# Non-final matmul chunks visit the PSUM banks in rotation instead of one bank after the other

## The chip, the cores and the metric

The kernel runs on one core of one Trainium2 chip, as one launch. The metric is the device time of that core in microseconds (us); lower is better. "TensorE" or PE is the matrix engine, VectorE is DVE, ScalarE is ACT, GpSimd is POOL and SyncE is SP. PSUM is the accumulator memory that TensorE writes; it has eight banks, and one bank takes an output of 128 x 512 f32.

## What is computed

One layer of a hybrid diffusion backbone: 256 latent tokens and 256 context tokens, model width 2048, everything in f32. Cut to what matters:

```
mod   = silu(c) @ w_mod + b_mod                          # shifts, scales, gates; w_mod 2048 x 12288
proj  = modulate(rms(x) * norm1, shift, scale) @ w_in    # w_in 2048 x 13376, latent and context rows
ssm   = rms(bidirectional_ssd(...) * silu(z)) @ w_ssm_br # 2048 x 2048
attn  = grouped_query_attention(q, k, v) @ w_attn_br     # 2048 x 2048
x_mid = x + gate1 * ((sigmoid(g1)*ssm + sigmoid(g2)*attn) @ w_o)
out   = x_mid + gate2 * (silu(h @ w_gate) * (h @ w_up)) @ w_ffn_out   # hidden width 5632
```

The large products dominate. Each is done with operands split in two, high and low part, and three products are summed: high*high + high*low + low*high. The change touches only the order in which these products are issued.

## The kernel before, in words

**Tiles and chunks.** A weight matrix is read in chunks of 1 MB: 512 columns by 512 rows, the rows lying as 4 tiles of 128 on the partitions (`CK_T` = 4). SP issues one DMA per chunk into one of 4 `raw` slots (L423). ACT makes the high part with one copy (L889, `w_hi`), DVE the low part with one subtraction (L1188, `w_lo`); both have two slots (`SPL` = 2), so chunk p+2 is split when chunk p is through on TensorE, which the semaphore `pe_used` tells. TensorE takes the activations (`act_hi`, `act_lo`, 128 tokens x 128 rows) as the stationary operand and the 512 weight columns as the moving one. Each matmul has its own weight load (LDWEIGHTS, shown as PEld).

**Blocks and banks.** A block is 512 output columns; it takes several chunks, and its sums stay in PSUM over all of them. Phases with latent tokens only have two 128-token tiles and so two banks per block (0 and 1); `kv`, `xb` and `dt` have latent and context tokens and so four banks. `br` and `f1` have two products per block, the first in banks 0 and 1 (chunks 0 to 3), the second in banks 2 and 3 (chunks 4 to 7). The phases in order, as blocks x chunks: kv 2x4, xb 6x4, dt 1x1, q 4x4, c 2x4, z 4x4 and g 8x4 (these two with modulation chunks and attention or SSD steps between), br 4x8, o 4x4, f1 11x8, f2 4x11. Before them stands the modulation phase with a function of its own (`mod_chunk`), which the change leaves alone.

**One chunk on TensorE** is the function `chunk` (L517 to L544): it waits for `hi_ready` and `lo_ready`, then loops over the banks, and for each bank over the 4 row tiles with 3 matmuls each: 12 matmuls per bank in a row (L539, L540, L541). So a chunk is 24 matmuls with two banks and 48 with four. In the first chunk of a block (`first`) the matmuls of each bank are preceded by a wait on `bank_free` (L532, or L530 in block 0, where only the first bank waits, for all earlier ones). In the last chunk (`final`) each bank but the last signals `bank_done` when its twelve are through; the last is told by `pe_used`.

**Evacuation.** After the first chunk of the next block has been split on that engine, the block's banks are copied out in order: by ACT in kv, xb, q, c, z, g (L897, `stage_out`), by DVE in br (L1519, `merge`), o (L1561, `residual`) and f2 (L1613, `finish`), and in f1 by ACT for banks 0 and 1 (L1138) and by DVE for banks 2 and 3 (L1589). Each copy raises `bank_free` by one.

**What sets the order.** Every engine's program is written out by hand in program order; nothing is scheduled by a planner. Waits hold an engine's whole queue.

Of the kernel before, what the change touches and what calls it, by code (L numbers as in the profile page):

```python
# [24 lines left out]
P = 128  # L25
# [70 lines left out]
def lin(values, i):  # L96

    if isinstance(i, int):
        return values[i]
    step = values[2] - values[1]  # L100
    assert all(b - a == step for a, b in zip(values[1:], values[2:]))
    return i * step + (values[1] - step)
# [12 lines left out]
def hybrid_block(nc, a, out):  # L115
    with ExitStack() as outer:
        def sem(name):
            return outer.enter_context(nc.semaphore(name))
# [62 lines left out]
        PS = outer.enter_context(nc.psum_tensor("PS", [P, 8, NB], F32))  # L181
# [96 lines left out]
        bank_done, bank_free = sem("bank_done"), sem("bank_free")  # L278
# [30 lines left out]
        def col(table, p):  # L309
            return [row[p] for row in table]  # L310
# [205 lines left out]
        def _(pe):  # L516
            def chunk(ph, i, p, acts, banks, kt0, first, final):  # L517

                pe.wait_ge(hi_ready, lin(col(ph.index, p), i) + 1)
                pe.wait_ge(lo_ready, lin(col(ph.index, p), i) + 1)  # L520
                s = p % SPL
                n, ks = (64, KT) if ph is p_dt else (NB, CK_T)
                hi_w = w_hi[:, s, :, :].rearrange("p k n -> p (k n)")[:, 0:ks * n].rearrange("p (k n) -> p k n", n=n)
                lo_w = w_lo[:, s, :, :].rearrange("p k n -> p (k n)")[:, 0:ks * n].rearrange("p (k n) -> p k n", n=n)
                for t, b in enumerate(banks):
                    if first:
                        prior = ph.banks.index(b) + 1
                        if isinstance(i, int) and i == 0:
                            if t == 0:
                                pe.wait_ge(bank_free, ph.bank0[0])  # L530
                        else:
                            pe.wait_ge(bank_free, lin(ph.bank0, i) - len(ph.banks) + prior)  # L532
                    dst = PS[:, b, 0:n]
                    toks = slice((t % 2) * P, (t % 2 + 1) * P)
                    for k in range(ks):
                        kt = kt0 + (16 if t >= 2 else 0) + k
                        x_hi, x_lo = acts[0][:, kt, toks], acts[1][:, kt, toks]
                        begin, end = first and k == 0, final and k == ks - 1
                        nc.tensor.matmul(dst, x_hi, hi_w[:, k, :], start=begin, stop=False)  # L539
                        nc.tensor.matmul(dst, x_hi, lo_w[:, k, :], start=False, stop=False)  # L540
                        last = nc.tensor.matmul(dst, x_lo, hi_w[:, k, :], start=False, stop=end)  # L541
                    if final and t < len(banks) - 1:
                        last.then_inc(bank_done, 1)
                last.then_inc(pe_used, 1)  # L544

            act1, act2 = (act1_hi, act1_lo), (act2_hi, act2_lo)
# [1 line left out]
            def plain(ph, i, p):  # L548
                chunk(ph, i, p, act1, ph.banks, p * CK_T, p == 0, p == ph.chunks - 1)
# [64 lines left out]
            for ch in range(4):  # L614
                for d in range(2):
# [3 lines left out]
                             start=True, stop=True).then_inc(d_pe, 1)  # L619
# [57 lines left out]
            def z_step(i):  # L677
                for p, what in enumerate(ORDER["z"]):
                    q = int(what[1])

                    if p == 2:
                        pe.wait_ge(a_qkS, i + 1)
                    if p >= 2:
                        attention_steps(i, p - 2, p - 1 if p < 11 else 11)
                    if what[0] == "m":
                        mod_chunk(p_z, i, p, i * 2 + (8 + q // 4), q % 4)
                    else:
                        chunk(p_z, i, p, act1, LAT, q * CK_T, q == 0, q == 3)
                    if p == 0 and not (isinstance(i, int) and i == 0):
                        mod_turn(i * 2 + 7)  # L690
                    if p == 6:
                        mod_turn(i * 2 + 8)
                    if p == 0:
                        attention_start(i)
# [76 lines left out]
            def g_step(i):  # L771
                conv_in(i)
                for p, what in enumerate(ORDER["g"]):
                    q = int(what[1])

                    if p in (1, 4, 6, 7):
                        {1: decays, 4: back_to_rows, 6: states, 7: outputs}[p](i)
                    if what[0] == "m":
                        mod_chunk(p_g, i, p, i + 16, q)
                    else:  # L780
                        chunk(p_g, i, p, act1, LAT, q * CK_T, q == 0, q == 3)
                    if p == 0:
                        mod_turn(i + 15)
# [876 lines left out]
```

## Time and profile before

| | |
|---|---|
| device time, median of 3 runs | 2692.27 us (2691.65 to 2692.89) |
| span of the profiled execution | 2691.1 us |
| TensorE busy (matmuls) | 2370.1 us, 88% of the span, 10239 matmuls |
| DVE / ACT / POOL busy | 1339.0 / 1057.4 / 71.5 us |
| the three matmul lines of `chunk` | 2592 matmuls each, 400 to 406 ns each |
| mean granted TensorE clock | 0.949 of full speed |
| HBM | 169 GB/s over the span |

How to read it: matmuls are pipelined, so a record of 0.40 us overlaps the next one. What counts is the distance from one start to the next, here called the pitch. A timeline row gives start, duration, engine, line, operation and operands; in brackets stands idle time before it and what ended it. A clock of 1.0 stands for 2.4 GHz and 0.5 for 1.2 GHz.

### The profile page before, as it was taken

Reading aid. Unit: us, or ns where it says so; the run is one execution under the profiler, and the core shown is the slowest. Engines: PE = TensorE matmul, PEld = TensorE weight load, DVE = VectorE, ACT = ScalarE, POOL = GpSimd, SP = SyncE. Lnnn points to the kernel's source line nnn. Section 1 sums busy time; section 2 is a strip of 40 time slices with the busy share of each in tenths; the row PEclk is TensorE's granted clock in tenths of the full one; section 3 lists DMA queues with packets and bytes.
Section 4 is the critical chain, followed back from the end, with each engine's and each line's share of the span. In section 5 each row is a group of like instructions: output and inputs, shape, how many; then the busy total and the mean of one; then the engine's idle time right before and its main releaser. Section 6 shows DMA issues by size and latency. Waiting matters only on the chain. (4 is left out here: it accounts for less than half of the span.)

```text
span 2691.1 us, 27845 instructions
## 1 busy us (share of the span) xinstructions
PE 2370.1 (88%) x10239; PEld 1865.6 (69%) x10239; DVE 1339.0 (50%) x1346; ACT 1057.4 (39%) x956; POOL 71.5 (3%) x111
## 2 busy tenths in 40 slices
PE   3689999979887877888778889999799999999999
PEld 2467888877655655666666667778688888877777
DVE  4752222123565555777676755554544444444333
ACT  4532222123355444444444434333444444443332
POOL 0000000000100001000000000000000000000000
PEclk9999999969989898999999989999899999999999
DMA  7933333216745555454444455645455555554553
GB/s 266 311 117 125 110 125 109 102 63 208 212 150 193 168 179 165 156 169 154 154 154 159 151 215 188 206 144 196 148 181 187 187 179 182 184 182 174 183 185 135
DMA packets 225435, 454.32 MB, mean 169 GB/s; under 512 B 11732, under 2 KB 14532, under 8 KB 224104
## 3 DMA queue, kind: packets, MB, share of 16 engines
q1 hardware_dynamic: 202704, 399.01, 43.2%
q0 software_dynamic: 8240, 32.12, 3.8%
q10 hardware_dynamic: 14440, 22.50, 2.3%
q8 instruction: 33, 0.54, 0.1%
q14 instruction: 18, 0.15, 0.0%
HBM read 429.47 MB, written 24.13 MB: 169 GB/s over the span
## 5 line engine op out<-in xcount | busy, mean ns | idle before, releaser
L1188 DVE TENSOR_TENSOR w_lo<-raw,w_hi 128x2048 fp32r<-128x2048 f32 x381 | 871.8, 2289 | 1008.6 <-ACT w_hi L889 1008.3
L539 PE MATMUL PS<-w_hi,act_hi 128*128 128x512 f32 (+1 forms) x2592 | 1051.7, 406 | 93.4 <-DVE w_lo L1188 60.6
L889 ACT ACTIVATE w_hi<-raw 128x2048 fp32r<-128x2048 f32 x381 | 726.9, 1910 | 902.0 <-PE PS L541 855.3
L540 PE MATMUL PS<-w_lo,act_hi 128*128 128x512 f32 (+1 forms) x2592 | 1037.5, 400 | 0.0
L541 PE MATMUL PS<-w_hi,act_lo 128*128 128x512 f32 (+1 forms) x2592 | 1035.8, 400 | 0.0
L539 PEld LDWEIGHTS PS<-w_hi,act_hi 128*128 128x128 f32 x2592 | 503.6, 194 | 239.8 <-issue 89.6
L541 PEld LDWEIGHTS PS<-w_hi,act_lo 128*128 128x128 f32 x2592 | 503.0, 194 | 119.1
L540 PEld LDWEIGHTS PS<-w_lo,act_hi 128*128 128x128 f32 x2592 | 503.7, 194 | 115.5 <-issue 1.7
L569 PE MATMUL PS<-w_hi,c 128*128 128x512 f32 x384 | 175.6, 457 | 117.3 <-DVE w_lo L1188 112.6
L569 PEld LDWEIGHTS PS<-w_hi,c 128*128 128x128 f32 x384 | 79.8, 208 | 163.5 <-issue 142.1
L570 PE MATMUL PS<-w_lo,c 128*128 128x512 f32 x384 | 165.2, 430 | 0.0
L570 PEld LDWEIGHTS PS<-w_lo,c 128*128 128x128 f32 x384 | 81.2, 211 | 16.6 <-issue 1.2
L1435 DVE SCALAR_TENSOR_TENSOR cv<-cin,conv_w,cv 128x256 f32<-128x256 f32 x224 | 91.5, 480 | 2.1 <-DVE cv L1433 0.2
L897 ACT ACTIVATE stage<-PS 128x512 f32<-128x512 f32 x68 | 39.2, 595 | 82.1 <-PE PS L541 80.7
L354 ACT ACTIVATE act_hi<-tmp 128x512 fp32r<-128x512 f32 x40 | 25.3, 632 | 84.5 <-DVE tmp L368 49.7
L1000 ACT ACTIVATE probs<-PS,ast 128x512 f32<-128x512 f32 x32 | 22.0, 689 | 74.0 <-DVE ast L1362 74.0
L738 PEld LDWEIGHTS PS<-tri,a_loc 128*128 128x128 f32 x256 | 33.6, 190 | 15.3 <-issue 15.3
L1065 ACT ACT_TABLE_LOAD x8 | 10.3, 1283 | 77.8 <-DVE cv L1435 77.7
L993 ACT ACTIVATE pT<-PS 128x512 f32<-128x512 f32 x32 | 19.1, 596 | 50.2 <-PE PS L637 50.2
L1484 DVE TENSOR_TENSOR dec<-PS,eacum 128x512 f32<-128x512 f32 x16 | 10.3, 687 | 56.4 <-PE PS L766 56.4
L647 PE MATMUL PS<-pT,vv 128*128 128x256 f32 x128 | 32.7, 401 | 4.0 <-ACT pT L993 4.0
L629 PE MATMUL PS<-kT,tmp 128*128 128x512 f32 x64 | 35.7, 641 | 0.0
(204 smaller groups left out, 1175.6 us busy)
## 6 DMA issues: line engine op xcount, KB each, us to landing
raw<-in_w_in SPq DMA_DIRECT2D x104, 1024.0 KB, 5.0
raw<-in_w_mod SPq DMA_DIRECT2D x96, 1024.0 KB, 5.1
raw<-in_w_ffn_in SPq DMA_DIRECT2D x88, 1024.0 KB, 4.9
raw<-in_w_ffn_out SPq DMA_DIRECT2D x44, 1024.0 KB, 5.1
raw<-in_w_attn_br SPq DMA_DIRECT2D x16, 1024.0 KB, 5.0
raw<-in_w_ssm_br SPq DMA_DIRECT2D x16, 1024.0 KB, 5.1
raw<-in_w_o SPq DMA_DIRECT2D x16, 1024.0 KB, 5.0
proj_lat<-stage ACTq DMA_DIRECT2D x52, 256.0 KB, 2.2
```

Of the source, the lines that this page charges most:

```text
L539: nc.tensor.matmul(dst, x_hi, hi_w[:, k, :], start=begin, stop=False)
L540: nc.tensor.matmul(dst, x_hi, lo_w[:, k, :], start=False, stop=False)
L541: last = nc.tensor.matmul(dst, x_lo, hi_w[:, k, :], start=False, stop=end)
L569: nc.tensor.matmul(PS[:, 7, :], cond, w_hi[:, p % SPL, k, :], start=(q == 0 and k == 0), stop=False)
L570: last = nc.tensor.matmul(PS[:, 7, :], cond, w_lo[:, p % SPL, k, :], start=False, stop=(q == 3 and k == CK_T - 1))
L629: nc.tensor.matmul(PS[:, 2 + u % 2, :], qT[:, h, t * P:(t + 1) * P], kT[:, :], start=True, stop=True).then_inc(a_sc, 1)
L647: last = nc.tensor.matmul(PS[:, 6, 0:T], vv[:, k, :], pT[:, h % 2, k, :], start=(k == 0), stop=(k == 3))
L738: last = nc.tensor.matmul(bank[:, h * P:(h + 1) * P], a_loc[:, c, d, h:h + 1].to_broadcast([P, P]), tri[:, d, :], start=False, stop=True, ...
L889: nc.scalar.activation(dst, src, ACT.Copy).then_inc(hi_ready, 1)
L897: nc.scalar.activation(stage[:, b, :], PS[:, bank, :], ACT.Copy).then_inc(bank_free, 1)
L1188: nc.vector.tensor_tensor(o, r, h, ALU.subtract).then_inc(lo_ready, 1)
L1435: ins = nc.vector.scalar_tensor_tensor(out=cv[:, m, :], in0=src, scalar=w, in1=cv[:, m, :], op0=ALU.mult, op1=ALU.add)
```

## The change

In a chunk that is not the last of its block's bank group, the loops are exchanged: the row tiles are outside, and for each row tile the high*high product goes to every bank, then the high*low product to every bank, then the low*high product to every bank. The products that one bank receives come in the same order as before, and their number is the same. The wait for `bank_free` of each bank now stands before that bank's first matmul in the first row tile, so all the waits come within the first two (or four) matmuls of the block. The last chunk keeps the old order. `pe_used` is still raised by the last matmul of the chunk. The whole diff:

```diff
--- before.py
+++ after.py
@@ -522,25 +522,43 @@
                 n, ks = (64, KT) if ph is p_dt else (NB, CK_T)
                 hi_w = w_hi[:, s, :, :].rearrange("p k n -> p (k n)")[:, 0:ks * n].rearrange("p (k n) -> p k n", n=n)
                 lo_w = w_lo[:, s, :, :].rearrange("p k n -> p (k n)")[:, 0:ks * n].rearrange("p (k n) -> p k n", n=n)
-                for t, b in enumerate(banks):
-                    if first:
-                        prior = ph.banks.index(b) + 1
-                        if isinstance(i, int) and i == 0:
-                            if t == 0:
-                                pe.wait_ge(bank_free, ph.bank0[0])
-                        else:
-                            pe.wait_ge(bank_free, lin(ph.bank0, i) - len(ph.banks) + prior)
-                    dst = PS[:, b, 0:n]
-                    toks = slice((t % 2) * P, (t % 2 + 1) * P)
+                def free(t, b):
+                    prior = ph.banks.index(b) + 1
+                    if isinstance(i, int) and i == 0:
+                        if t == 0:
+                            pe.wait_ge(bank_free, ph.bank0[0])
+                    else:
+                        pe.wait_ge(bank_free, lin(ph.bank0, i) - len(ph.banks) + prior)
+
+                def operands(t, k):
+                    kt, toks = kt0 + (16 if t >= 2 else 0) + k, slice((t % 2) * P, (t % 2 + 1) * P)
+                    return acts[0][:, kt, toks], acts[1][:, kt, toks]
+
+                if final:
+                    for t, b in enumerate(banks):
+                        if first:
+                            free(t, b)
+                        for k in range(ks):
+                            x_hi, x_lo = operands(t, k)
+                            dst, begin, end = PS[:, b, 0:n], first and k == 0, k == ks - 1
+                            nc.tensor.matmul(dst, x_hi, hi_w[:, k, :], start=begin, stop=False)
+                            nc.tensor.matmul(dst, x_hi, lo_w[:, k, :], start=False, stop=False)
+                            last = nc.tensor.matmul(dst, x_lo, hi_w[:, k, :], start=False, stop=end)
+                        if t < len(banks) - 1:
+                            last.then_inc(bank_done, 1)
+                else:
                     for k in range(ks):
-                        kt = kt0 + (16 if t >= 2 else 0) + k
-                        x_hi, x_lo = acts[0][:, kt, toks], acts[1][:, kt, toks]
-                        begin, end = first and k == 0, final and k == ks - 1
-                        nc.tensor.matmul(dst, x_hi, hi_w[:, k, :], start=begin, stop=False)
-                        nc.tensor.matmul(dst, x_hi, lo_w[:, k, :], start=False, stop=False)
-                        last = nc.tensor.matmul(dst, x_lo, hi_w[:, k, :], start=False, stop=end)
-                    if final and t < len(banks) - 1:
-                        last.then_inc(bank_done, 1)
+                        for t, b in enumerate(banks):
+                            if first and k == 0:
+                                free(t, b)
+                            x_hi = operands(t, k)[0]
+                            nc.tensor.matmul(PS[:, b, 0:n], x_hi, hi_w[:, k, :], start=first and k == 0, stop=False)
+                        for t, b in enumerate(banks):
+                            x_hi = operands(t, k)[0]
+                            nc.tensor.matmul(PS[:, b, 0:n], x_hi, lo_w[:, k, :], start=False, stop=False)
+                        for t, b in enumerate(banks):
+                            x_lo = operands(t, k)[1]
+                            last = nc.tensor.matmul(PS[:, b, 0:n], x_lo, hi_w[:, k, :], start=False, stop=False)
                 last.then_inc(pe_used, 1)
 
             act1, act2 = (act1_hi, act1_lo), (act2_hi, act2_lo)
```

## Rows read from the trace of the kernel before

**Rows 1.** Page, parts 1 and 4: engine busy time; the chain that ended last.
```profile
PE 2370.1 (88%) x10239; PEld 1865.6 (69%) x10239; DVE 1339.0 (50%) x1346; ACT 1057.4 (39%) x956; POOL 71.5 (3%) x111
...
PE PS L539 9%; PE PS L540 9%; PE PS L541 9%; ACT w_hi L889 0%; PE PS L841 0%; DVE w_lo L1188 0%; DVE tmp L368 0%; DVE stage L1613 0%; DVE act_lo L1593 0%; DVE stage L1616 0%; ACT act_hi L1142 0%; DVE stage L1589 0%; PE PS L346 0%; DVEq L1615 0%; DVEq L321 0%
```

**Rows 2.** Waits view, whole run: waiter, releaser: us in total, times, longest.
```profile
PE PS L539 <- DVE w_lo L1188: 60.6, 37, 4.3
```

**Rows 3.** Timeline of TensorE, phase f1, across bank switches at 2003.50 and 2006.30.
```profile
2000.70 0.39 PE L539 MATMUL PS<-w_hi,act_hi 128*128 128x512 f32 x1
...
2003.26 0.40 PE L541 MATMUL PS<-w_hi,act_lo 128*128 128x512 f32 x1
2003.50 0.39 PE L539 MATMUL PS<-w_hi,act_hi 128*128 128x512 f32 x1
...
2006.30 0.39 PE L539 MATMUL PS<-w_hi,act_hi 128*128 128x512 f32 x1
```

**Rows 4.** Timeline, phase xb, start of block 1 (its first matmul is at 301.51).
```profile
301.51 0.40 PE L539 MATMUL PS<-w_hi,act_hi 128*128 128x512 f32 x1
301.71 0.60 ACT L897 ACTIVATE stage<-PS 128x512 f32<-128x512 f32 x1 [2.20 <-PE PS L541]
```

**Rows 5.** Timeline, phase q, start of block 1 (first matmul at 607.48).
```profile
607.48 0.39 PE L539 MATMUL PS<-w_hi,act_hi 128*128 128x512 f32 x1
607.67 0.60 ACT L897 ACTIVATE stage<-PS 128x512 f32<-128x512 f32 x1 [2.10 <-PE PS L541]
```

**Rows 6.** Timeline, phase q, from chunk 0 to chunk 1 of block 1.
```profile
610.96 2.29 DVE L1188 TENSOR_TENSOR w_lo<-raw,w_hi 128x2048 fp32r<-128x2048 f32 x1 [4.64 <-ACT w_hi L889]
...
612.84 0.39 PE L541 MATMUL PS<-w_hi,act_lo 128*128 128x512 f32 x1
...
613.40 0.47 PE L539 MATMUL PS<-w_hi,act_hi 128*128 128x512 f32 x1 [0.17 <-DVE w_lo L1188]
...
613.70 0.39 PE L540 MATMUL PS<-w_lo,act_hi 128*128 128x512 f32 x1
```

**Rows 7.** Timeline, phase c, block 1: TensorE before chunk 2, and DVE's reduction.
```profile
714.20 0.48 PE L539 MATMUL PS<-w_hi,act_hi 128*128 128x512 f32 x1 [3.49 <-DVE w_lo L1188]
...
710.10 1.75 DVE L1317 TENSOR_REDUCE ast<-qk_sq 128x12 f32<-128x1536 f32 x1
711.77 2.28 DVE L1188 TENSOR_TENSOR w_lo<-raw,w_hi 128x2048 fp32r<-128x2048 f32 x1
```

**Rows 8.** Timeline, phase o, start of block 2 (first matmul at 1841.66).
```profile
1841.66 0.40 PE L539 MATMUL PS<-w_hi,act_hi 128*128 128x512 f32 x1
...
1841.86 0.69 DVE L1561 TENSOR_TENSOR tmp<-PS,gt 128x512 f32<-128x512 f32 x1 [0.76 <-PE PS L541]
```

**Rows 9.** Chain that ended last, phase f2, start of block 2: start, us, what.
```profile
2553.19 0.69 DVE stage L1613
2553.93 0.79 PE PS L539
2554.72 0.43 PE PS L540
```

**Rows 10.** Timeline, phase f2, start of block 2: the second bank's evacuation, TensorE.
```profile
2553.79 0.68 DVE L1613 TENSOR_TENSOR stage<-PS,tmp 128x512 f32<-128x512 f32 x1
...
2554.52 0.63 PE L540 MATMUL PS<-w_lo,act_hi 128*128 128x512 f32 x1
```

**Rows 11.** Timeline, evacuations in br and f1, and br's first matmul of block 1.
```profile
1640.74 1.28 DVE L1519 TENSOR_TENSOR wide<-PS,gates 128x512 f32 x2
...
1642.44 0.79 PE L539 MATMUL PS<-w_hi,act_hi 128*128 128x512 f32 x1
...
1998.53 1.09 ACT L1138 ACTIVATE stage<-PS 128x512 f32<-128x512 f32 x2
```

**Rows 12.** Windows view: window, us, busy by engine, granted clock, DMA share, GB/s.
```profile
604.00:616.00 12.00, 11.83 (x51) 9.27 (x50) 5.37 (x3) 5.03 (x4) 0.00 (x0) 1.00 0.63 208
...
2552.00:2558.00 6.00, 4.07 (x10) 3.25 (x11) 5.90 (x5) 0.75 (x1) 1.27 (x2) 0.52 0.54 178
```

## Prediction, made before the changed kernel was run

> **What bounds the kernel now.** I began with the page's busy shares and its chain [rows 1]: TensorE is busy 88% of the span and the lines of the chain that weigh anything are the three matmul lines of `chunk`, so a time added to or taken from those matmuls counts in full wherever TensorE runs without a gap. Then the waits [rows 2]: TensorE waits for the weight split only 60.6 us in all in these lines, in a few places. Then the timeline inside a chunk, which gives the price of one matmul [rows 3]: the twelve matmuls of one bank go from 2000.70 to 2003.50, the next twelve from 2003.50 to 2006.30, 2.80 us each, a pitch of 233.3 ns. Last, the timeline at the start of each block, phase by phase, because that is where the change moves waits [rows 4 to 11].
>
> **Pitch.** The non-final chunks, whose order changes, hold 288 + 864 + 288 + 144 + 288 + 576 + 576 + 288 + 1584 + 960 = 5856 matmuls (kv, xb, q, c, z, g, br, o, f1, f2; e.g. xb: 6 blocks x 3 chunks x 48). Nothing is removed or added: as many matmuls, weight loads and semaphore signals. What changes is that each matmul now writes another bank than the one before it. The trace of before already has such switches: the one at 2003.50 comes 0.24 us after the matmul before it, and both stretches of twelve, each with one switch, take the same 2.80 us [rows 3]. So a bank switch costs nothing that the rows can show; they are printed to 0.01 us, so the bound is +-10 ns per switch. Of the 5856, z and g (864) stand in phases with gaps of many us around them; on the rest, 4992, the bound would be +-50 us. I take 0, since the row is the very operation and shows no step. The rotation also keeps the moving operand and changes the stationary one between neighbours; before, the high*high to high*low step keeps the stationary one and the low*high to next high*high step changes both, and the stretches of 2.80 us average over these. Cost taken: 0.
>
> TensorE's clock: the pitch at the half level (0.52 granted in the window that holds it [rows 12]) is 2554.95 - 2554.52 = 0.43 us [rows 9, 10], which is 512 columns at 1.2 GHz; at the full level half of that would be 213.3 ns, and the trace has 233.3. So 20 ns per matmul are not the columns. The Trainium skill, "TensorE: Matmul & The Clock Gate", section "Wait — 56ns, not 53.3ns?", gives a start-to-start of 215.7 ns for 512 columns, which this trace does not reach. If chaining into one bank were what costs the difference, the page's figure would give 4992 x 17.6 ns = 88 us back. The switch row speaks against it; it is a rival below.
>
> **The moved waits.** In a block's first chunk, the wait for the second bank stood 12 matmuls (2.80 us) after the first matmul; now it stands one matmul (0.23 us) after it, and with four banks the last stands 0.70 us after it instead of 8.4 us. The last bank of the block before can be evacuated only after the block's last matmul, so its copy starts about 0.20 us into the new block. What the cover of 2.80 us hid now shows. Two restart prices: from an evacuation's end to the released weight load 0.05 us (2553.88 to 2553.93 [rows 9]); and from a matmul whose weight load was held to the next one 0.30 us instead of 0.23 us (613.40 to 613.70 [rows 6]). Behind the held load everything on TensorE's queue stands, and `pe_used` and all later chunks with it. Times below are for one boundary; the others of the phase have the same rows within 0.01 us.
>
> - kv and xb, four banks, ACT copies: the fourth copy ends at 301.71 + 0.60 = 302.31 [rows 4]. Held matmul 302.36, the next 302.66; without the hold that one comes at 301.51 + 4 x 0.233 = 302.44. Cost 0.22 us, taken 0.23, at 1 + 5 boundaries: 1.38 us. (Block 0 of any phase waits once for all banks before its first matmul, so nothing moves there.)
> - q, two banks: copy ends at 607.67 + 0.60 = 608.27 [rows 5], held matmul 608.32, next 608.62, against 607.48 + 0.467 = 607.94. Gross 0.68 us. But chunk 1 of such a block is late today for another reason: its weight split ends at 610.96 + 2.29 = 613.25, it starts at 613.40, its second matmul is at 613.70 where 612.84 + 0.467 = 613.31 was due [rows 6], 0.39 us late. The split hangs on the end of the block before, not on chunk 0. With chunk 0 later by 0.68 us the split is in time (613.25 against 613.76), so 0.39 us vanish: net 0.29 us, x 3 = 0.87 us.
> - c, one boundary, gross the same 0.68 us: absorbed. Chunk 2 of that block waits 3.49 us for its split at 714.20, and DVE makes that split at the end of a run of its own work (710.10 + 1.75, then 711.77) that began with the split of chunk 1 and never waits for chunk 0 [rows 7]. Cost 0; all of it up to 0.6 us if I misread that run.
> - o, DVE copies: 1841.86 + 0.69 = 1842.55 [rows 8], held matmul 1842.60, next 1842.90 against 1841.66 + 0.467 = 1842.13: 0.77 to 0.78 us x 3 = 2.34 us. No later wait in the block is due.
> - f2: DVE comes late to both banks, so TensorE already waits for the first copy. The second ends at 2553.79 + 0.68 = 2554.47, held matmul 2554.52, which is just when it runs today [rows 10]; only the restart is new. At this clock it is (2554.52 - 2553.93) - 0.43 = 0.16 us [rows 9, 10], x 3 = 0.48 us.
> - br, f1, z, g: nothing. In br and f1 both copies end before the block's first matmul: br 1642.02 against 1642.44, f1 1999.62 against 2000.70 [rows 11, 3]; the second pair of banks is needed four chunks later. In z and g a modulation chunk or two stands on TensorE between a block's last chunk and the next block's first, and the copies are done under it. If this cover were gone at the 23 boundaries (br 3, f1 10, z 3, g 7), each would cost what o's does, 18 us; nothing in the rows takes it away.
>
> Sum: 1.38 + 0.87 + 0 + 2.34 + 0.48 = 5.07 us on the profiled execution, 2691.1 to 2696.2. The median of the runs is 1.2 us above that span, so 2692.27 + 5.07 = 2697.3 us.
>
> Ends of the unknown costs: if no restart is paid, only the copies' ends count: kv and xb 6 x 0.10, q 3 x 0.17, o 3 x 0.66, f2 0, together 3.1 us. If a release costs 0.15 us (split's end 613.25 to matmul 613.40 [rows 6]) in place of 0.05, 12 to 15 x 0.10 more, and c's 0.6 us too, 7 us.
>
> **Rivals.**
> 1. *The same-bank chain costs the 20 ns.* For it: the pitch is above its columns only at the full clock, and all matmuls of a chunk but one are chained. Against: the switched matmul comes no sooner [rows 3]. 4992 x 20 ns = 100 us less, plus the 5 us of waits: 2597 us. The split would still keep up (1.92 + 2.29 us of ACT and DVE against 24 x 0.213 = 5.1 us per chunk). This is the faster side.
> 2. *The new stops drop the clock.* Place: the 12 stops in kv, xb, q and o; it decides if a stop of 0.6 us is enough. Price: after f2's stop of 5.3 us the clock was 0.52 over 2552 to 2558, and some 9 matmuls ran at 0.43 instead of 0.23 us [rows 9, 12], 1.8 us; x 12 = 22 us, so 2719 us. Against: q already has a stop of 0.57 us (612.84 to 613.40 instead of 0.23 later) and the window 604 to 616 around it shows 1.00 [rows 6, 12]. The Trainium skill speaks for it: the same page, section "A second HAM failure mode: psum-queue depth-cycling", says that going through PSUM banks in each iteration makes TensorE idle in small pieces so often that its clock swings between both levels. No run here shows that yet; row 6 and its window disagree for a single short stop.
> 3. *Less is seen of the stops than I sum*: TensorE loses no restart, 3.1 us, 2695.4 us.
> 4. *A small price or gain per bank switch*, under what the rows resolve: 2 ns either way is 10 us: 2707 or 2687 us.
>
> **How the numbers follow.** Forecast 80%: 2697.3, between 2695.7 and 2699.2. Rival 3: 5%. Rival 1: 4%. Rival 2: 4%. Rival 4: 4% slower, 3% faster. The range 2694.5 to 2700.5 holds the forecast and rival 3, with 0.7 us for the spread of the runs; the 15% of the others stay out. A change of 0.2%, 5.4 us, is about what a measurement of this kernel can tell from none; the line is at 2697.65, just above my number. So the 80% splits, 36 slower and 44 same. Slower 0.36 + 0.04 + 0.04 = 0.44; same 0.44 + 0.05 = 0.49; faster 0.04 + 0.03 = 0.07.
>
> **What would show it.** Right: matmul pitch still 233 ns in rotated chunks; a new wait of TensorE's weight loads for ACT's L897 copies (9 or 10 times) and DVE's o copies (3 times); the gap before q's chunk 1 gone; the 3.49 us wait in c shorter by about 0.7 us; f1 as long as before. Wrong: any other pitch, a stop at the start of an f1 or br block, or a half clock in xb or o.

## The result, and the profile after

The changed kernel takes 2699.33 us (median of 11 runs, 2694.51 to 2701.27) against 2692.27 us (11 runs, 2688.08 to 2695.37): 7.1 us more, ratio 1.0025 with a 95% interval of 1.0017 to 1.0033. The profiled execution has a span of 2699.5 us, that of before 2691.1. The likeliest case of the forecast was 5.07 us over before, 2697.3 us, range 2694.5 to 2700.5. It gave "within 0.2%" a little more chance than "slower by over 0.2%"; the measured ratio lies just on the other side of that line, with an interval that reaches over to both sides.

From the page of the changed kernel, busy time by engine and two of the rotated lines (busy us, mean ns, idle before): as many matmuls and weight loads as before [rows 1], at the same 400 ns each.

```profile
PE 2378.0 (88%) x10239; PEld 1868.8 (69%) x10239; DVE 1339.1 (50%) x1346; ACT 1057.5 (39%) x956; POOL 71.6 (3%) x111
...
L558 PE MATMUL PS<-w_lo,act_hi 128*128 128x512 f32 x1952 | 608.0, 401 | 0.0
L561 PE MATMUL PS<-w_hi,act_lo 128*128 128x512 f32 x1952 | 606.2, 400 | 0.0
```

**The pitch has not moved.** Timeline of TensorE in q, block 1, from the first chunk into the second, and DVE's split for the second (start, us). Each row is two matmuls, one per bank:

```profile
611.22 0.63 PE L555 MATMUL PS<-w_hi,act_hi 128*128 128x512 f32 x2
611.69 0.63 PE L558 MATMUL PS<-w_lo,act_hi 128*128 128x512 f32 x2
...
612.62 0.63 PE L555 MATMUL PS<-w_hi,act_hi 128*128 128x512 f32 x2
...
609.78 2.29 DVE L1206 TENSOR_TENSOR w_lo<-raw,w_hi 128x2048 fp32r<-128x2048 f32 x1 [4.64 <-ACT w_hi L907]
```

From 611.22 to 612.62 are six matmuls in 1.40 us: 233.3 ns, with a bank switch at each, as with one switch in twelve before [rows 3]. The same rows show that q's chunk 1 now starts without a gap: its split is ready at 609.78 + 2.29 = 612.07, and the late start of before [rows 6] is gone.

**New waits.** Waits view of the changed kernel: who waited, for whom, us in total, times, longest. In the view of before, TensorE's weight loads have no row for these copies, and the matmuls only the 3.1 us at the first blocks of phases.

```profile
PEld PS L555 <- ACT stage L915: 6.1, 10, 0.9
PE PS L555 <- ACT stage L915: 4.2, 7, 0.8
PEld PS L555 <- DVE tmp L1579: 3.0, 3, 1.0
```

Ten loads wait for ACT's copies (kv 1, xb 5, q 3, c 1), three for DVE's in o. The timelines at three block starts (start, us; in brackets idle before and its end), first xb block 1 (four banks), to be held against [rows 4]:

```profile
300.66 1.35 PE L555 MATMUL PS<-w_hi,act_hi 128*128 128x512 f32 x4
300.86 0.60 ACT L915 ACTIVATE stage<-PS 128x512 f32<-128x512 f32 x1 [2.20 <-PE PS L546]
...
301.85 1.08 PE L558 MATMUL PS<-w_lo,act_hi 128*128 128x512 f32 x4
```

then q block 1, against [rows 5], and o block 2, against [rows 8]:

```profile
606.50 0.60 ACT L915 ACTIVATE stage<-PS 128x512 f32<-128x512 f32 x1 [2.11 <-PE PS L546]
...
607.15 0.50 PE L555 MATMUL PS<-w_hi,act_hi 128*128 128x512 f32 x1 [0.46 <-ACT stage L915]
...
607.49 0.63 PE L558 MATMUL PS<-w_lo,act_hi 128*128 128x512 f32 x2
```

```profile
1847.26 0.40 PE L555 MATMUL PS<-w_hi,act_hi 128*128 128x512 f32 x1
...
1847.46 0.69 DVE L1579 TENSOR_TENSOR tmp<-PS,gt 128x512 f32<-128x512 f32 x1 [0.76 <-PE PS L546]
1848.20 0.50 PE L555 MATMUL PS<-w_hi,act_hi 128*128 128x512 f32 x1 [0.55 <-DVE tmp L1579]
...
1848.54 0.63 PE L558 MATMUL PS<-w_lo,act_hi 128*128 128x512 f32 x2
```

In each, TensorE does one matmul per free bank, then stands until the last bank's copy has ended (301.46, 607.10, 1848.15). The held matmul starts 0.05 us after that end and the next one 0.34 us later (in xb the held one is the fourth of the first row, at 301.51). In o, the third matmul comes at 1848.54 where 1847.26 + 0.467 = 1847.73 was due: 0.81 us.

Below, a block start's cost is the time from the last matmul start of one chunk to that of the next, read from both traces and subtracted. For the changed kernel:

| block starts | forecast each | measured each | forecast sum | measured sum |
|---|---|---|---|---|
| kv 1, xb 5 (11.20 us before) | 0.23 | 0.25 | 1.38 | 1.51 |
| q 3, first chunk (5.60 before) | 0.68 | 0.71 to 0.72 | | |
| q 3, second chunk (5.97 to 6.00 before) | -0.39 | -0.37 to -0.40 | 0.87 | 1.00 |
| o 3 (5.60 before) | 0.78 | 0.81 | 2.34 | 2.44 |
| f2 3 (12.75, 12.53, 12.33 before) | 0.16 | 0.34, 0.19, 0.18 | 0.48 | 0.71, a part of it by the clock |
| br, f1, z, g | 0 | 0 | 0 | 0 (but see the clock) |
| sum | | | 5.07 | 5.66 |

### The profile page after: what moved, and what is told of

The parts are those of the page before. It is cut to its first block and busy times, and to the rows that moved or that the text cites. A ratio compares the mean times of both kernels' runs of the same rounds, so it can differ in the third digit from the quotient of the medians.

```text
span 2699.5 us, 27845 instructions
## 1 busy us (share of the span) xinstructions
PE 2378.0 (88%) x10239; PEld 1868.8 (69%) x10239; DVE 1339.1 (50%) x1346; ACT 1057.5 (39%) x956; POOL 71.6 (3%) x111
## 5 line engine op out<-in xcount | busy, mean ns | idle before, releaser
L555 PE MATMUL PS<-w_hi,act_hi 128*128 128x512 f32 x1952 | 625.5, 409 | 76.4 <-DVE w_lo L1206 41.1
L558 PE MATMUL PS<-w_lo,act_hi 128*128 128x512 f32 x1952 | 608.0, 401 | 0.0
L561 PE MATMUL PS<-w_hi,act_lo 128*128 128x512 f32 x1952 | 606.2, 400 | 0.0
L544 PE MATMUL PS<-w_hi,act_hi 128*128 128x512 f32 (+1 forms) x640 | 257.8, 403 | 18.8 <-DVE w_lo L1206 18.0
L545 PE MATMUL PS<-w_lo,act_hi 128*128 128x512 f32 (+1 forms) x640 | 255.0, 398 | 0.0
L546 PE MATMUL PS<-w_hi,act_lo 128*128 128x512 f32 (+1 forms) x640 | 254.6, 398 | 0.0
L915 ACT ACTIVATE stage<-PS 128x512 f32<-128x512 f32 x68 | 39.2, 595 | 85.1 <-PE PS L546 83.7
```

What stands on the lines that cost most here:

```text
L555: nc.tensor.matmul(PS[:, b, 0:n], x_hi, hi_w[:, k, :], start=first and k == 0, stop=False)
L558: nc.tensor.matmul(PS[:, b, 0:n], x_hi, lo_w[:, k, :], start=False, stop=False)
L561: last = nc.tensor.matmul(PS[:, b, 0:n], x_lo, hi_w[:, k, :], start=False, stop=False)
L915: nc.scalar.activation(stage[:, b, :], PS[:, bank, :], ACT.Copy).then_inc(bank_free, 1)
```

## The experiments

**Theory A**: all of the cost is the waits that moved forward in a block's first chunk. **Theory B**: rotation itself costs, in pitch or clock, wherever it is done. The first four kernels ran on one chip, where before is 2691.98 us (24 runs).

**e1_later_only.** The first chunks keep the old order, the others rotate:

```
-                if final:
+                if final or first:
```

(`stop` and `bank_done` stay with `final`, as in the kernel before.)

> The first chunk of each block keeps the old order, all other non-final chunks rotate. Theory A (the moved waits cost everything): every block start as before the change (xb 11.20 us per first chunk, o 5.60 us), total as before, within 1.5 us. Theory B (rotation itself costs, in matmul pitch or clock): most of the changed kernel's +7 us stays.

Measured: 2692.62 us, ratio 1.0001 (0.9992 to 1.0010). Phase by phase the trace is that of before within 0.05 us, except a g that starts 0.22 us sooner and is 0.17 us longer. In the waits view the row for ACT's copies is that of before again, and there is none for o:

```profile
PE PS L544 <- ACT stage L915: 3.1, 4, 0.8
```

Two thirds of the rotation cost nothing. B has fallen for them.

**e2_first_only.** The other half: only first chunks rotate (`if final or not first:`).

> Only the first chunk of each block rotates, the middle chunks keep the old order. Theory A: the block starts cost what they cost in the changed kernel (xb +0.25, q +0.71 and -0.38 one chunk later, o +0.81, f2 +0.2 to +0.3), in sum 5.7 us, total +5.7 to +7. Theory B: less than a third of the changed kernel's cost, under 2.5 us, since only 2000 or so of the 5856 matmuls rotate.

Measured: 2701.03 us, ratio 1.0030 (1.0018 to 1.0043). The block starts cost xb 0.25, q 0.71 to 0.73, o 0.81 to 0.82, f2 0.33, 0.19 and 0.17 us: those of the changed kernel to 0.02 us. One part does not repeat: the second chunk of q's block 1 takes 0.14 us more than before instead of 0.40 less, because its split is ready late again. In e8 and e10 it is -0.22 and -0.09, and in e7, which has the old order, +0.50; so this one row changes from trace to trace whatever the order. The cost sits in the first chunks.

**e3_after_again.** The changed kernel, a second trace.

> The changed kernel once more, for a second trace of it. Its first trace has 8.4 us more than that of before, of which the block starts explain 5.7; the rest lies in c (+1.5) and g (+3.2) less 2 us elsewhere. Theory A with chance in how the clock's low stretches fall: the block starts repeat within 0.02 us, while c and g come out otherwise. Theory C (a real cost in c and g): c +1.5 and g +3.2 again.

Measured: 2699.91 us, ratio 1.0030 (1.0019 to 1.0041); span 2696.9 us, 2.5 us below the first trace. The block starts repeat within 0.03 us. c is as long as before (+0.01 instead of +1.47), g is 0.29 us shorter instead of 3.25 longer, z 0.99 longer instead of 0.10. Theory C, a fixed cost in c and g, has fallen.

**e4_czg_only.** Rotation in c, z and g alone (`if final or not (ph in (p_c, p_z, p_g)):`).

> Rotation only in c, z and g. Theory A: c's one stop of 0.7 us is absorbed by the wait before its chunk 2 and z and g have none, total as before within 1.5 us. Theory C: c and g cost +3 to +5 us by themselves.

Measured: 2693.46 us, ratio 1.0005 (0.9996 to 1.0014), not to be told from none. In the trace c's stop of 0.71 us is there and is swallowed: the late start of chunk 1 (-0.14) goes, and chunk 2 comes when DVE's split comes. z and g are within 0.3 us of before; c is 1.55 us longer by the clock, as the part on e9 shows.

**e5_double_new and e6_double_old.** The same edit in the changed order and in the old one: in kv, xb, q, c and o the last bank of a block is copied twice before it is freed (the extra copy goes to a buffer that nobody reads). For ACT:

```
+                    if b == len(ph.banks) - 1 and ph.name in ("kv", "xb", "q", "c"):
+                        nc.scalar.activation(res4[:, :], PS[:, bank, :], ACT.Copy)
                     nc.scalar.activation(stage[:, b, :], PS[:, bank, :], ACT.Copy).then_inc(bank_free, 1)
```

and for DVE in o the same product into `diag` first.

> Changed order, and in kv, xb, q, c (ACT) and o (DVE) the last bank of a block is copied twice before it is freed, the first copy into a buffer nobody reads. Two copies in a row take 1.09 us instead of 0.60 on ACT and 1.28 instead of 0.69 on DVE in the trace of before. Theory A (the copy of the last bank sets the stop): each block start grows by just that: xb from +0.25 to +0.74 us, q from +0.71 to +1.20 (chunk 1 then in time, -0.38), o from +0.81 to +1.41, in sum 12 us over before. Rival (a fixed price per early wait, whatever the copy takes): block starts as in the changed kernel, 5.7 us.

> Old order with the same doubled copies. Theory A: the 2.80 us of matmuls before the second wait hide 1.5 us as they hide 1.0: xb and o block starts 0, only q's chunk 1 is later by 0.49 us in each of 3 blocks, 1.5 us in all. Rival: the doubled copies cost the same in both orders.

Measured on one chip (before 2692.62 us): new order 2708.34 us, ratio 1.0058 (1.0041 to 1.0075); old order 2696.93 us, ratio 1.0013 (1.0004 to 1.0023). The block starts in the new order are xb 0.73 to 0.74, q 1.20 to 1.21 and -0.37 to -0.40, o 1.41 us, as forecast. In the old order kv's, xb's and o's cost nothing, q's second chunk 0.43 to 0.45. The totals are higher than forecast in both (15.7 and 4.3 us by the medians). A part of that I had left out: the first matmul of a phase waits for all banks at once, so the doubled copy shows there in either order (xb, dt, c and z 0.48 to 0.50 us each in both traces, and f1, which starts behind o's last copy, 0.96), 2.9 us in all. The timelines at o block 2, new order and then old order:

```profile
1852.13 0.39 PE L555 MATMUL PS<-w_hi,act_hi 128*128 128x512 f32 x1
...
1852.33 0.69 DVE L1582 TENSOR_TENSOR diag<-PS,gt 128x512 f32<-128x512 f32 x1 [0.76 <-PE PS L546]
1852.93 0.68 DVE L1584 TENSOR_TENSOR tmp<-PS,gt 128x512 f32<-128x512 f32 x1
1853.67 0.51 PE L555 MATMUL PS<-w_hi,act_hi 128*128 128x512 f32 x1 [1.15 <-DVE tmp L1584]
```

```profile
1845.76 0.39 PE L539 MATMUL PS<-w_hi,act_hi 128*128 128x512 f32 x1
...
1845.96 0.69 DVE L1564 TENSOR_TENSOR diag<-PS,gt 128x512 f32<-128x512 f32 x1 [0.76 <-PE PS L541]
...
1846.57 0.68 DVE L1566 TENSOR_TENSOR tmp<-PS,gt 128x512 f32<-128x512 f32 x1
1846.70 0.39 PE L540 MATMUL PS<-w_lo,act_hi 128*128 128x512 f32 x1
1846.93 0.40 PE L541 MATMUL PS<-w_hi,act_lo 128*128 128x512 f32 x1
1847.16 0.39 PE L539 MATMUL PS<-w_hi,act_hi 128*128 128x512 f32 x1
```

The stop follows the copy's length in the new order. In the old one TensorE runs on beside both copies, which end at 1847.25, before the twelve matmuls from 1845.76 on are through. This shows the cover of twelve matmuls directly.

**e7_f2_turn_old and e8_f2_turn_new.** In f2 the change was cheap because DVE was late to both banks. Here that lateness is taken away in either order: f2 is written out block by block, and its slots (the `raw` ones likewise) go on alternating across the border:

```
+def turn(ph, i, p):
+    return (i * ph.chunks if ph.name == "f2" else 0) + p
...
-                s = p % SPL
+                s = turn(ph, i, p) % SPL
```

> Old order; f2 is written out block by block so that its 11 chunks go on alternating between the slots over the block borders (before, chunk 10 and the next chunk 0 share a slot, so the split waits). The 5.3 us stops before three f2 blocks go, and the matmuls at the half clock behind them (9 x 0.19 us): 3 x 6.9 = 21 us less than before, about 2671 us.

> The same f2 with the changed order. Theory A: DVE is now in time at f2's block starts, which then are like o's: +0.81 us each instead of +0.2 to +0.3. So 5.7 - 0.7 + 2.4 = 7.4 us over the same f2 in old order. Rival (f2's price is its own): +0.2 to +0.3 each, 5.7 us over it.

Measured, same chip as e5 and e6 (four runs each): old order 2671.12 us, ratio 0.9922 (0.9905 to 0.9938); new order 2679.40 us, ratio 0.9950 (0.9933 to 0.9966). The difference is 8.3 us. All three f2 block starts take 5.60 us in the old order (12.3 to 12.8 before) and 6.41 us in the new: +0.81 us, o's price. f2 block 2 in the new order:

```profile
2547.47 0.39 PE L566 MATMUL PS<-w_hi,act_hi 128*128 128x512 f32 x1
2547.67 0.69 DVE L1644 TENSOR_TENSOR stage<-PS,tmp 128x512 f32<-128x512 f32 x1 [0.70 <-PE PS L557]
...
2548.42 0.50 PE L566 MATMUL PS<-w_hi,act_hi 128*128 128x512 f32 x1 [0.55 <-DVE stage L1644]
2548.76 0.63 PE L569 MATMUL PS<-w_lo,act_hi 128*128 128x512 f32 x2
```

So f2's small price was the work of another lateness and not of f2. The old order with this f2 is faster than both kernels, by 21 us than the one before.

**e9_o_first_only and e10_all_but_f1.** In each trace with rotated first chunks, f1's very first chunk takes 0.44 to 0.45 us more (in e5 1.8, of which 0.96 is a later start of f1 behind the doubled copy, as in e6), though it has no new wait. Is it the rotation in f1, or that o before it is longer? Here the chunks rotate only where `ph is p_o and first` (e9) or `ph is not p_f1` (e10); one run each.

> Only o's first chunks rotate. In all four traces with rotated first chunks f1's first chunk takes 0.45 us more, with 10 or 11 matmuls at the half clock instead of 8. Theory A (o is 2.4 us longer, so the clock's low stretch falls otherwise on f1's start): o +2.44 us and f1's first chunk +0.45 again, all else as before. Theory D (rotation in f1 does it): f1 as before.

> The changed kernel with the old order in all of f1. Theory A: f1's first chunk still takes 0.45 us more than before. Theory D: it takes the time of before. In both f1's other chunks stay at 5.60 us.

Measured: both +0.44 to +0.45 us in f1's first chunk (the single runs took 2697.52 us in e9 and 2700.28 us in e10, against one run of before at 2697.08; one run is too few for a ratio). In e10 f1 has the old order throughout. TensorE's timeline from f1's first matmul on, before and then e10:

```profile
1905.31 0.77 PE L539 MATMUL PS<-w_hi,act_hi 128*128 128x512 f32 x1 [3.87 <-DVE w_lo L1188]
...
1908.86 0.59 PE L541 MATMUL PS<-w_hi,act_lo 128*128 128x512 f32 x1
1909.29 0.39 PE L539 MATMUL PS<-w_hi,act_hi 128*128 128x512 f32 x1
```

```profile
1911.56 0.76 PE L544 MATMUL PS<-w_hi,act_hi 128*128 128x512 f32 x1 [3.87 <-DVE w_lo L1206]
...
1915.96 0.63 PE L545 MATMUL PS<-w_lo,act_hi 128*128 128x512 f32 x1
1916.39 0.46 PE L546 MATMUL PS<-w_hi,act_lo 128*128 128x512 f32 x1
1916.68 0.39 PE L544 MATMUL PS<-w_hi,act_hi 128*128 128x512 f32 x1
```

The half clock (0.43 us from start to start) lasts for 3.98 us of f1 before and for about 4.9 us in e10. The windows view of both, with the granted clock third from the right, shows where that comes from. The first two rows are of before, the others of e10; o's last matmul starts at 1886.23 and at 1892.47:

```profile
1886.30:1888.70 2.40, 0.32 (x2) 0.00 (x0) 1.92 (x2) 0.06 (x1) 0.00 (x0) 1.00 0.00 0
1888.80:1909.20 20.40, 7.88 (x25) 6.14 (x26) 11.23 (x16) 11.41 (x12) 0.73 (x1) 0.50 0.39 154
...
1892.60:1895.90 3.30, 0.27 (x2) 0.00 (x0) 1.92 (x2) 1.01 (x1) 0.59 (x1) 1.00 0.00 0
1896.10:1916.40 20.30, 8.83 (x28) 6.81 (x29) 12.02 (x17) 10.49 (x12) 0.00 (x0) 0.50 0.41 155
```

TensorE stands idle after o, and the clock falls 2.6 us after o's last matmul before and 3.5 us after it in e10. It stays low equally long, about 20.5 us, and f1 starts 19.1 us after o's last matmul in both. So the low stretch is not longer; it lies 1 us later against the work, and f1 gets 1 us more of it. At the half clock 1 us does the work of 0.55 (233 against 427 ns a matmul), which is the 0.45 us. In every trace whose o is 2.4 us longer the fall comes 3.5 us after its last matmul, in every one whose o is as before 2.6 us, and in e5, whose o is 4.45 us longer, 5.4 us. A longer o suffices (e9). Why the fall comes later by just that much is not shown. The 0.45 us belong to the change, but through the clock.

The same happens in f2, which e9 leaves alone: its block starts take 0.25, 0.13 and 0.00 us more than before. Block 1 in before, in the changed kernel and in e9, in this order (first matmul of the block, third matmul, and in before and e9 the first one after the clock has risen):

```profile
2485.18 0.79 PE L539 MATMUL PS<-w_hi,act_hi 128*128 128x512 f32 x1 [4.93 <-DVE stage L1613]
...
2486.20 0.63 PE L541 MATMUL PS<-w_hi,act_lo 128*128 128x512 f32 x1
...
2489.59 0.39 PE L540 MATMUL PS<-w_lo,act_hi 128*128 128x512 f32 x1
```

```profile
2492.86 1.40 PE L555 MATMUL PS<-w_hi,act_hi 128*128 128x512 f32 x2 [4.93 <-DVE stage L1631]
2494.05 1.05 PE L558 MATMUL PS<-w_lo,act_hi 128*128 128x512 f32 x2
```

```profile
2489.44 0.80 PE L544 MATMUL PS<-w_hi,act_hi 128*128 128x512 f32 x1 [4.92 <-DVE stage L1631]
...
2494.30 0.42 PE L546 MATMUL PS<-w_hi,act_lo 128*128 128x512 f32 x1
```

The third matmul comes 1.19 us after the first in the changed kernel and 1.02 us before: the restart, 0.17 us. But the clock rises 4.4 us after the block's first matmul before, and 4.9 us after it in the changed kernel and in e9, where no wait of f2 has moved.

e9 had also a surprise: c, untouched there, is 1.54 us longer than before. Its last chunk meets a low stretch:

```profile
722.98 0.63 PE L544 MATMUL PS<-w_hi,act_hi 128*128 128x512 f32 x1
723.40 0.63 PE L545 MATMUL PS<-w_lo,act_hi 128*128 128x512 f32 x1
```

where the same chunk of before runs at 0.23 us a matmul. So c's +1.5 us comes with and without the change (with it in three traces, not in e3, e5, e8 or e10; without it in e9): it comes and goes from trace to trace.

## Why the prediction was right, point by point

**Pitch: right.** The one switch in twelve that the trace of before contained told what a switch at each matmul would cost: nothing, 233.3 ns in both. Rivals 1 and 4 have fallen with it. The reordering of what stays stationary cost nothing either. The 20 ns over the columns' time are there with and without a chain into one bank; what they are stays open.

**The moved waits: right in place and, to about a tenth, in size.** Every phase named has its stop and none has one elsewhere; q's absorption and c's came as worked out. The mis-sized term outside f2 is the restart. I took 0.30 us from the held to the next matmul, from a wait for a weight split [rows 6]; after a wait for a bank it is 0.34 us, which gives the 0.02 to 0.04 us too little of each row of the table, 0.36 us in all outside f2. In f2 the restart itself was forecast well: 0.17 us measured in blocks 1 and 2, 0.16 forecast. The sum there is 0.23 us too small by what the forecast left out, the place of the clock's low stretches. They lie 0.5 and 0.2 us later against blocks 1 and 2, as in e9, which adds 0.24 and 0.08 us (an estimate from the two pitches; e9 measures 0.25 and 0.13 with f2 untouched). The other way, a stop inside a low stretch that ends when it would have ended anyway costs only 0.55 of its length, so each restart costs about 0.09 us (an estimate from the same pitches). Block 3 was misread: in before its second matmul comes 0.45 us after the first (2622.46 to 2622.91), not 0.59 as in blocks 1 and 2, so the prediction's "same rows within 0.01 us" does not hold there, and the held copy costs 0.15 us beside the restart. Together 0.59 us: 5.66 instead of 5.07.

**What was not in the sum.** I set the clock's part at zero except in rival 2. Rival 2 as I put it has fallen: around the stops of xb the clock is 1.00, and so it is around those of xb, q and o in e5, which are longer (windows view: window, us, busy by engine, granted clock, DMA share, GB/s; the first row is of the changed kernel, the others are of e5).

```profile
255.00:525.00 270.00, 269.22 (x1150) 214.91 (x1150) 53.95 (x24) 59.49 (x48) 0.00 (x0) 1.00 0.32 108
...
255.00:525.00 270.00, 266.35 (x1137) 212.26 (x1136) 53.95 (x24) 61.80 (x53) 0.00 (x0) 1.00 0.31 103
600.00:684.00 84.00, 81.17 (x346) 64.36 (x345) 33.28 (x15) 32.49 (x24) 0.00 (x0) 1.00 0.60 194
1808.00:1899.00 91.00, 87.20 (x379) 69.20 (x378) 47.39 (x39) 29.14 (x18) 0.00 (x0) 1.00 0.50 173
```

With it goes, for this kernel, the warning of the Trainium skill, "TensorE: Matmul & The Clock Gate", section "A second HAM failure mode: psum-queue depth-cycling", that cycling through banks makes the clock swing: rotation alone makes no idle piece (e1), and stops of up to 1.15 us (e5, o) drew no low stretch. But the low stretches that the kernel has anyway shift against the work when something before them gets longer. f1's 0.45 us is such a term, and reproducible. The medians of the changed kernel are 7.1 us (first comparison) and 7.9 us (e3's chip) over before, 5.66 + 0.45 = 6.1 us are accounted for by rows, and the intervals of both ratios reach from 1.0017 and 1.0019 up, that is from 4.6 and 5.1 us. The remaining 1 to 2 us may be such shifts in dt, q, c, z and g, or nothing. In the single traces what is left beside the block starts and f1 lies between 2.0 us less (e7) and 2.3 us more (changed kernel, e2) than in that of before, and 0.2 us less in e3. That is not settled. So the median is 2.0 us above the likeliest case: 0.6 us by the terms above, 0.45 us by f1's clock, and about 1 us unexplained, which the range was wide enough to hold.

**Rival 3** (no restart paid) has fallen: the restart is in every row. **The chances**: the place of the 0.2% line between my number and the measured one made "same" or "slower" a near toss, and a sum with the true restart and f1's clock, 6.1 us, would have put slower first.

**The observations listed ahead** came out so: loads waiting for L915's copies 10 times and for o's 3 times; the gap before q's chunk 1 gone; c's wait before chunk 2 shorter; f1's other chunks as long as before. Only f1's first chunk was not foreseen.

## What to carry to other kernels

An order of matmuls is also an order of waits. Going round the banks in the inner loop puts the wait for the last bank, whose copy cannot start before the block before has ended, one matmul after the block's start instead of twelve (with four banks three instead of 36), and uncovers the copy. The price here is the 0.2 us until the copy starts, plus the copy (0.6 to 0.7 us), plus 0.16 us of release and restart, less the 0.23 us of each matmul that is issued meanwhile: 0.73 us for q, 0.82 for o, 0.26 for xb, with 0.71, 0.81 and 0.25 measured. To price it, look in the trace of before at when the last bank's copy ends against the new place of its wait, and at what is late right behind it: a later wait can swallow the stop (q by half, c wholly), and a lateness before it can hide it (f2). Ask also which stretches at the half clock follow, and whether a longer phase moves them against the work (f1, f2). Rotation that starts only in the second chunk costs nothing, and here it also gained nothing.

## What was not expected of the hardware

- After a matmul whose weight load was held for a bank the next matmul starts 0.34 us later, when the pitch is 0.23 us (0.30 us after a wait for a weight split); with the 0.05 us from the copy's end, each stop is 0.16 us longer than the copy alone explains (1848.15 to 1848.20 to 1848.54).
- A 2.4 us longer phase o put the half-clock stretch behind it 1 us later against the work, without making it longer: the clock falls 3.5 instead of 2.6 us after o's last matmul and is low for about 20.5 us in both. f1 then runs 4.9 instead of 3.98 us at the half clock, 0.45 us of time, in every trace with such an o. In c, z and g the low stretches fell otherwise from trace to trace: c +1.5 us or 0, also with unchanged code (e9).
- A stop inside a low stretch costs less than its length: f2's restart of 0.17 us costs about 0.09 us (an estimate from 233 and 427 ns a matmul), because the clock rises when it would have risen anyway.
